# Joint last column tiles of two projections, rows reloaded into places that come free, and other places for the sample steps, in a one-core decoder layer on Trainium2

## The chip, the cores and the metric

The kernel runs on one core of one Trainium2 chip. The metric is the device time of one execution in microseconds (us). Execution is launched once; everything below happens inside it.

A core has TensorE (PE in the profile, its weight loads PEld), VectorE (DVE), ScalarE (ACT), GpSimd (POOL) and SyncE (SP). Each engine runs its own program in order; they meet through semaphores, with `wait_ge` on one side and `then_inc` on the other. DMA transfers are issued from an engine's queue and signal a semaphore when they land.

## The reference, cut to what matters

All data is float32. There are 1024 prompt rows and 8 sample rows, together R = 1032 rows of D = 2048 columns.

```python
h = rms_norm(x, g_mix);  z = h @ w_in
oa = three dilated windows of 16 heads, mixed by their softmax denominators
ob = sliding window of 128 keys, 16 query / 4 kv heads, sink logits
y = concat(oa * silu(ga), ob * silu(gb))                   # 2048 columns
h = x + y @ w_out
gate = sigmoid(rms_norm(h, g_ple) @ w_pg)
out = rms_norm(h + (p @ w_ple) * gate, g_final)            # p has 256 columns
# the 8 sample rows attend to caches: cache_a (2048 positions), cache_b (128 positions)
```

w_in has 6656 columns, that is NZ = 52 tiles of 128; `ORDER` lists them in the order in which they are computed.

## The kernel before, in words

**Products.** Each product of float32 matrices is made of three products of rounded parts: an activation tile is split into a high part (`act_hi`, rounded) and a low part (`act_lo`, the rest), and so is each weight. `three()` (line 809) issues for one k (one of KT = 16 row blocks of the weights) the products hi*hi, lo*hi and hi*lo of 344 rows into a PSUM bank. The 1032 rows are three stretches of 344 (t = 0, 1, 2), so a column tile is 3 x 16 x 3 = 144 products. A pair (tile, t) is a unit. The step of one k of one unit is a position: position 16u + k.

**Weights.** SP loads a group of four k of a tile (256 KB) into one of two raw places (`weights(g)`, line 261); GpSimd rounds it and subtracts (lines 575 and 577) into one of five places of a ring (`WRING`). It waits for the place to be used up. There are 208 groups for w_in and 64 for w_out. The gate's weights w_pg and w_ple have places of their own (`u_even`, `u_odd`, line 229), are loaded a whole tile at a time (`load_u`, line 519) and are split by VectorE (`split_u`, line 1381).

**First projection** (line 818). Units run one after the other through PSUM banks 0 and 1. ScalarE copies a unit out (line 948) or, for the 16 gating tiles from unit GATE0 = 108 on, takes its silu (line 955); VectorE multiplies that by the attention output (line 1311) and SP stores the product to DRAM (`yt_scratch`, line 457).

**Work beside it.** The attention of the prompt, the sample rows' attention A (`sa`, eight sequences) and B (`sb`) run between the products of the first projection. The table in `events()` (line 68) says at which position each step stands. Every engine walks the same list in order of position (`ALONG`): TensorE executes a step's matmuls when it reaches the position, SP issues that step's loads, VectorE and ScalarE do their parts. So a step's wait on TensorE holds up all later products, and a step's wait on SP holds up all later loads. For each sequence b of sample attention A the steps stand at 1448 + 96b plus an offset: key and value loads (`sa_load`, line 386), VectorE's scores (`sk`, line 1225), TensorE's steps 1 to 5 (`sa_step`, line 723). For attention B the rows are turned at 2226, TensorE turns each sequence's scores at 2250 + 14b as VectorE delivers them (line 779), and the steps 1 to 4 stand at 2370, 2400, 2420 and 2440. The projection ends at position 2496.

**Second projection** (line 840). When the last unit's y is stored, SP loads all 16 row blocks of y back into four places (`y_in`, line 502), ScalarE rounds each (line 1062), VectorE subtracts (line 1364), and TensorE computes tile 0 with k outermost, behind them. Tiles 1 to 15 then run unit by unit. Every unit ends with three small matmuls that add the residual x (`residual`, line 833). ScalarE copies h out and stores it (line 1071); VectorE adds up the squares of h over the 16 tiles in `acc` (lines 1369 and 1371).

**Gate stage.** After the last tile: TensorE sums `acc` over the partitions with a matrix of ones (line 870), VectorE adds eps (1376), ScalarE takes the root (1077), VectorE inverts (1379). Meanwhile SP loads h back (line 528), ScalarE scales and rounds (1081), VectorE subtracts (1390), and in between TensorE turns the nine row tiles of p (line 877). Then each of 16 column tiles has three units of 48 + 6 products (gate, then embedding, lines 886 to 888) and a turn of the previous unit's result (line 898); VectorE and ScalarE form h + ple * gate, and GpSimd issues the stores to `y_scratch` (lines 584 and 585).

**Last stage.** SP loads nine row tiles of y (line 552) into three places; ScalarE squares, VectorE scales into one of two places `f_out`, GpSimd issues the store of the output (line 589). ScalarE's next square but one into the same place waits for that store.

## Time and profile before

| | us |
|---|---|
| median of 3 runs | 2685.92 (2680.72 to 2686.15) |
| the profiled execution's own time | 2688.74 |
| its span, first to last instruction | 2686.9 |
| PE busy | 2468.8 (92%) |
| DVE, ACT, POOL busy | 861.3, 610.3, 621.5 |
| mean granted TensorE clock | 0.958 |

The span is that of the profiled execution. Products overlap in the pipeline, so the duration shown for one is longer than the distance from one start to the next; the distance is what counts. The stretches of the span are: up to 66 us the input norm and turn; 66 to 1727.6 the first projection; 1727.6 to 1767.6 the first tile of the second; to 2138.8 its other tiles; to 2190.6 the way into the gate stage and its first unit; to 2604.9 the gate stage; then the last stage.

### The profile page before, as it was taken

To read this page: it belongs to the slowest core of one execution; us is meant where nothing else is said; L and a number is where in the kernel's file an instruction comes from. 1 tells how busy PE (TensorE), PEld (TensorE's weight loads), DVE (VectorE), ACT (ScalarE), POOL (GpSimd) and SP (SyncE) were. 2 spreads that over 40 slices of the span, in tenths; PEclk is the share of its full clock that TensorE was granted. 3 is DMA by queue.
4 is the path that set the end of the run, shared out by engine and by line. 5 is a ranking of instruction groups with operands and counts; after the bars stand their busy time and mean duration, and the time that the engine had idled before them with its cause. 6 is when DMAs were issued, how large, how long until landed. Compare 5 with 4: busy or idle time off the path is not lost.

```text
span 2686.9 us, 40432 instructions
## 1 busy us (share of the span) xinstructions
PE 2468.8 (92%) x16617; PEld 2298.9 (86%) x16617; DVE 861.3 (32%) x2136; ACT 610.3 (23%) x1458; POOL 621.5 (23%) x653
## 2 busy tenths in 40 slices
PE   4999999999999999999899887899999969999970
PEld 3998888888888898888788887799999859999970
DVE  7022332332332304445544223231101163323224
ACT  5022222222222213335454000120000131101013
POOL 2222222222222232222111321234333201111110
PEclk7999999999999999999999998899999979999995
DMA  4132222232322234434443442443323253232326
GB/s 170 57 117 93 87 91 91 91 97 85 96 90 83 70 99 133 136 112 131 143 121 116 130 142 76 135 145 95 89 75 90 78 184 96 73 96 74 94 70 235
DMA packets 301962, 287.95 MB, mean 107 GB/s; under 512 B 20865, under 2 KB 267449, under 8 KB 298425
## 3 DMA queue, kind: packets, MB, share of 16 engines
q1 hardware_dynamic: 278898, 241.11, 29.8%
q10 hardware_dynamic: 17856, 27.34, 3.0%
q0 software_dynamic: 5024, 16.92, 1.7%
q8 instruction: 132, 2.16, 0.3%
q14 instruction: 52, 0.43, 0.1%
HBM read 215.48 MB, written 69.81 MB: 106 GB/s over the span
## 4 chain that ended last, share of the span: by engine, by line
PE 83%; DVE 7%; DMA 6%; ACT 2%; issue 1%; POOL 1%; SPq 1%; POOLq 0%; DVEq 0%; ACTq 0%
PE psum L813 18%; PE psum L815 17%; PE psum L814 17%; PE psum L886 5%; PE psum L888 5%; PE psum L887 5%; PE psum L618 3%; PE psum L634 3%; PE psum L646 3%; DMA s_ring<-in_cache_a_v 1%; PE psum L837 1%; DMA out<-f_out 1%; PE psum L674 1%; DMA s_ring<-in_cache_a_k 1%; PE psum L689 1%
## 5 line engine op out<-in xcount | busy, mean ns | idle before, releaser
L813 PE MATMUL psum<-act_hi,w_hi 128*128 128x344 f32 x3264 | 1078.9, 331 | 14.1 <-DVE act_lo L1364 13.1
L815 PE MATMUL psum<-act_hi,w_lo 128*128 128x344 f32 x3264 | 1051.9, 322 | 0.0
L814 PE MATMUL psum<-act_lo,w_hi 128*128 128x344 f32 x3264 | 1051.5, 322 | 0.0
L813 PEld LDWEIGHTS psum<-act_hi,w_hi 128*128 128x128 f32 x3264 | 623.6, 191 | 25.7 <-issue 20.1
L814 PEld LDWEIGHTS psum<-act_lo,w_hi 128*128 128x128 f32 x3264 | 622.7, 191 | 0.0
L815 PEld LDWEIGHTS psum<-act_hi,w_lo 128*128 128x128 f32 x3264 | 622.1, 191 | 0.0
L575 POOL CAST w_hi<-w_raw 128x512 fp32r<-128x512 f32 x272 | 182.4, 671 | 1547.9 <-PE psum L815 1406.6
L577 POOL TENSOR_TENSOR w_lo<-w_raw,w_hi 128x512 fp32r<-128x512 f32 x272 | 366.5, 1348 | 21.8
L1162 DVE COPY prob_t<-psum 128x512 f32<-128x512 f32 (+2 forms) x96 | 53.5, 558 | 470.0 <-PE psum L646 470.0
L584 POOL DMA_DIRECT2D y_scratch<-y_nat x48 | 36.7, 764 | 425.1 <-ACT y_nat L1092 415.5
L886 PE MATMUL psum<-act_hi,u_even 128*128 128x344 f32 x384 | 125.5, 327 | 9.4 <-DVE u_even L1387 8.3
L970 ACT ACTIVATE prob<-prob,mx 128x256 f32<-128x256 f32 (+7 forms) x128 | 98.4, 770 | 145.8 <-DVE mx L1190 145.8
L1184 DVE CUSTOM_DVE_ANT_0 prob<-psum,bias 128x512 f32<-128x512 f32 (+2 forms) x192 | 98.7, 552 | 94.9 <-PE psum L618 94.9
L964 ACT ACTIVATE prob_t<-psum 128x512 f32<-128x512 f32 (+2 forms) x96 | 47.2, 492 | 353.6 <-PE psum L646 353.6
L1369 DVE TENSOR_TENSOR sq<-h_row 128x1032 f32<-128x1032 f32 x16 | 21.3, 1332 | 326.9 <-ACT h_row L1071 326.9
L886 PE MATMUL psum<-act_hi,u_odd 128*128 128x344 f32 x384 | 124.6, 325 | 0.0
L888 PE MATMUL psum<-act_hi,u_even 128*128 128x344 f32 x384 | 123.1, 321 | 0.0
L887 PE MATMUL psum<-act_lo,u_even 128*128 128x344 f32 x384 | 123.0, 320 | 0.0
L888 PE MATMUL psum<-act_hi,u_odd 128*128 128x344 f32 x384 | 122.5, 319 | 0.0
L887 PE MATMUL psum<-act_lo,u_odd 128*128 128x344 f32 x384 | 122.5, 319 | 0.0
L1095 ACT ACTIVATE t_gate<-t_gate 128x344 f32<-128x344 f32 x48 | 23.6, 492 | 374.0 <-DVE t_gate L1407 374.0
L1407 DVE TENSOR_TENSOR t_gate<-psum,acc 128x344 f32<-128x344 f32 x48 | 24.8, 517 | 252.4 <-PE psum L888 252.4
(198 smaller groups left out, 2742.1 us busy)
## 6 DMA issues: line engine op xcount, KB each, us to landing
w_raw<-in_w_in SPq DMA_DIRECT2D x208, 256.0 KB, 3.0
w_raw<-in_w_out SPq DMA_DIRECT2D x64, 256.0 KB, 2.8
u_raw<-in_w_pg SPq DMA_DIRECT2D x16, 1024.0 KB, 6.3
z_scratch<-stage ACTq DMA_DIRECT2D x72, 172.0 KB, 1.8
h_scratch<-h_row ACTq DMA_DIRECT2D x16, 516.0 KB, 3.3
h_stage<-h_scratch SPq DMA_DIRECT2D x16, 516.0 KB, 4.7
h_in<-h_scratch SPq DMA_DIRECT2D x48, 172.0 KB, 2.6
x_in<-in_x_prompt SPq DMA_DIRECT2D x8, 1024.0 KB, 5.1
```

The lines of the kernel that those rows point to most:

```text
L575: pool.tensor_copy(w_hi[:, slot], w_raw[:, g % 2]).then_inc(sem("w_rounded"), 1)
L577: pool.tensor_tensor(w_lo[:, slot], w_raw[:, g % 2], w_hi[:, slot].bitcast(F32), ALU.subtract).then_inc(sem("w_split"), 1)
L618: pe.matmul(psum[:, 2 + h, 0:nk], zq[half, b * BLK:(b + 1) * BLK], zk[half, n_ % 2, k0:k0 + nk], start=True, stop=True).then_inc(sem("a_sc ...
L634: mm = pe.matmul(psum[HD * h:HD * h + HD, 6, (b % 4) * P:(b % 4 + 1) * P], v_nat[:, k0 // P + x, HD * h:HD * h + HD], prob_t[:, h, x * P:( ...
L813: pe.matmul(psum[:, bank, 0:T3], w_hi[:, slot, x, :], act_hi[:, k, rows], start=(k == 0), stop=False, skip_group_check=True)
L814: pe.matmul(psum[:, bank, 0:T3], w_hi[:, slot, x, :], act_lo[:, k, rows], start=False, stop=False, skip_group_check=True)
L815: return pe.matmul(psum[:, bank, 0:T3], w_lo[:, slot, x, :], act_hi[:, k, rows], start=False, stop=stop, skip_group_check=True)
L886: pe.matmul(psum[:, bank, 0:T3], hi_w[:, first + k, :], hi_a[:, k, rows], start=(k == 0), stop=False, skip_group_check=True)
L887: pe.matmul(psum[:, bank, 0:T3], hi_w[:, first + k, :], lo_a[:, k, rows], start=False, stop=False, skip_group_check=True)
L888: mm = pe.matmul(psum[:, bank, 0:T3], lo_w[:, first + k, :], hi_a[:, k, rows], start=False, stop=(k == tiles - 1), skip_group_check=True)
L970: act.activation(pr, pr, ACT.Exp, bias=mx[:, b % 4, 4 + h:5 + h], accum_out=mx[:, b % 4, 6 + h:7 + h]).then_inc(sem("a_exped"), 1)
L1184: dve.tensor_tensor_reduce(prob_of(n, b)[:, h, k0:k0 + nk], psum[:, 2 + h, 0:nk], bias[:, h, u0:u0 + nk], SCALE, -3e38, ALU.add, ALU.max, ...
```

## The change

**Joint tiles.** The last two tiles of the first projection, and the last two of the second, are computed with k outermost: for each k both tiles, all three stretches, in six PSUM banks. When both have used a k of the old activations, a semaphore (`x_used`, `yk_used`) says so, and ScalarE and VectorE write the reloaded rows of the next stage into that place of `act_hi` and `act_lo`. So 14 of the 16 blocks of y are reloaded while the pair of the first projection runs, and 14 of h while that of the second runs; the last two come from PSUM and from `h_row` directly, not through DRAM. `y_in` and `h_stage` have three places instead of four.

**Sample steps.** The pair needs banks 0 to 5, so the sample attention has to be over at position 2400 (`sb_done`). Steps of A stand at 1448 + 88b with other offsets; B's begin at 2160; TensorE turns all eight sequences' scores together at step 1 (position 2330), with one wait. Steps 2 to 4 stand at 2350, 2366 and 2382.

**Weights.** All weights, w_pg and w_ple too, go through GpSimd's ring of five as one list of groups (`GROUPS`, `USES`); a tile of the gate stage has four groups of four k and one of two. VectorE's split is gone.

**Gate stage.** Tile 0 is computed with k outermost in banks 4 to 6. The sums over the partitions come within it (after k = 11 and k = 14). The turns of p are put behind tiles 1 to 9 of the second projection. Turned results go to banks 3 and 7.

**Queues.** The stores of `y_scratch` and of the output are issued by ScalarE instead of GpSimd. The load of `g_ple` (4-byte elements) moves from before the gate stage to the kernel's beginning, ahead of `g_mix`.

```diff
@@ events
-    for b in range(NB):
-        first = 1448 + 96 * b
-        for i, at in enumerate((0, 1, 14, 18, 30, 76)):
+        first = 1448 + 88 * b
+        for i, at in enumerate((0, 1, 16, 22, 34, 72)):
             put(first + at, "sa_load", b, i)
-        for t, at in enumerate((8, 13, 24)):
+        for t, at in enumerate((8, 13, 26)):
             put(first + at, "sk", b, t)
-        for step, at in ((1, 34), (2, 54), (3, 72), (4, 84), (5, 94)):
+        for step, at in ((1, 42), (2, 58), (3, 70), (4, 83), (5, 87)):
             put(first + at, "sa", b, step)
-    put(2226, "sb_rows")
-    put(2240, "sb", 0)
-        put(2250 + 14 * b, "sb_seq", b)
-    put(2370, "sb", 1)  # 2400, 2420, 2440: 2, 3, 4
+    put(2160, "sb_rows")
+    put(2174, "sb", 0)
+        put(2184 + 14 * b, "sb_seq", b)
+    put(2330, "sb", 1)  # 2350, 2366, 2382: 2, 3, 4
@@ TensorE
+            pe.wait_ge(sem("bank_free"), ZPAIR)
+            pe.wait_ge(sem("sb_done"), 1)
+            for k in range(KT):
+                for i in range(2):
+                    group_wait("in", NZ - 2 + i, k)
+                    for t in range(3):
+                        mm = three(3 * i + t, "in", NZ - 2 + i, k, t, k == KT - 1)
...
+                    if k < KT - 1 and i == 1:
+                        mm.then_inc(sem("x_used"), 1)
...
+                if k == 11:
+                    pe.wait_ge(sem("h_summed"), 3 * KT)
+                    mean_square(0)
+                    mean_square(1)
+                elif k == 14:
+                    pe.wait_ge(sem("h_eps"), 1)
+                    mean_square(2)
@@ ScalarE
+            for k in range(HPAIR):
+                act.wait_ge(sem(f"y_loaded{k % 3}"), 16 * (k // 3 + 1))
+                act.wait_ge(sem("x_used"), k + 1)
+                act.activation(act_hi[:, k, 0:S], y_in[:, k % 3, :], ACT.Copy).then_inc(sem("y_hi"), 1)
+            act.wait_ge(sem("y_split"), HPAIR)
+            for j in range(2):
+                act.wait_ge(sem("produced"), ZPAIR + 3 * j + 3)
+                act.activation(gs[:, HPAIR + j, :], psum[:, 3 * j + 2, S - 2 * T3:T3], ACT.Silu).then_inc(sem("gs_gated"), 1)
...
+                act.wait_ge(sem("f_scaled"), i + 1)
+                act.dma_start(yp[r0:r0 + n, :] if i < 8 else ys, f_out[0:n, i % 2, :]).then_inc(sem(f"out_stored{i % 2}"), 16)
@@ GpSimd
-            for g in range(WG * NT):
+            for g, (what, i, k, n) in enumerate(GROUPS):
...
-                pool.dma_start(y_dram[q0:q0 + 256, n * P:(n + 1) * P].rearrange("(c p) n -> p c n", p=P), y_nat[:, u % 2, 0:2, :]).then_inc(sem(f"y_stored{u % 2}"), 16)
```

## Rows read from the trace of the kernel before

**Rows 1.** Stretch, length; busy PE, PEld, DVE, ACT, POOL; clock, DMA share, GB/s.

```profile
1050.00:1556.00 506.00, 477.42 (x3302) 420.63 (x3301) 221.03 (x759) 196.99 (x523) 115.11 (x120) 0.97 0.43 126
1556.00:1705.00 149.00, 123.32 (x759) 118.77 (x758) 44.17 (x81) 11.88 (x25) 35.81 (x38) 0.91 0.35 108
1727.60:1767.60 40.00, 26.86 (x145) 25.32 (x145) 25.24 (x22) 17.48 (x18) 8.20 (x7) 0.83 0.82 264
2138.80:2190.60 51.80, 19.84 (x79) 14.40 (x80) 36.76 (x35) 25.38 (x31) 0.00 (x0) 0.60 0.79 246
2190.60:2604.90 414.30, 414.30 (x2679) 413.47 (x2679) 133.63 (x171) 42.56 (x137) 68.04 (x90) 1.00 0.28 80
2604.90:2686.90 82.00, 0.91 (x7) 0.39 (x5) 30.16 (x57) 22.92 (x35) 8.61 (x15) 0.52 0.62 226
```

**Rows 2.** TensorE's waits: line, releaser, us in total, times, longest.

```profile
PE psum L779 <- DVE bsc L1334: 19.5, 6, 7.1
PE psum L719 <- DMA s_ring<-in_cache_a_v: 14.6, 8, 3.7
PE psum L727 <- DVE s_sc L1239: 10.3, 5, 3.2
PE psum L785 <- DVE bprob L1303: 6.2, 1, 6.2
```

**Rows 3.** Timeline of TensorE, products after a wait: start, duration.

```profile
1577.10 0.49 PE L814 MATMUL psum<-act_lo,w_hi 128*128 128x344 f32 x1
1577.39 0.49 PE L815 MATMUL psum<-act_hi,w_lo 128*128 128x344 f32 x1
...
1680.56 0.32 PE L814 MATMUL psum<-act_lo,w_hi 128*128 128x344 f32 x1
1680.71 0.32 PE L815 MATMUL psum<-act_hi,w_lo 128*128 128x344 f32 x1
```

**Rows 4.** Chain of waits: a value load of sample attention A.

```profile
1410.83 3.88 DMA s_ring<-in_cache_a_v
```

**Rows 5.** Groups of instructions: count, busy, mean ns, idle before.

```profile
L577 POOL TENSOR_TENSOR w_lo<-w_raw,w_hi 128x512 fp32r<-128x512 f32 x272 | 366.5, 1348 | 21.8
L575 POOL CAST w_hi<-w_raw 128x512 fp32r<-128x512 f32 x272 | 182.4, 671 | 1547.9 <-PE psum L815 1406.6 <-DMA w_raw<-in_w_in 113.2 <-DMA w_raw<-in_w_out 27.4
L1379 DVE RECIPROCAL acc<-acc 128x344 f32<-128x344 f32 x3 | 6.6, 2262 | 0.0
L877 PE MATMUL psum<-ident,y_nat 128*128 128x128 f32 (+1 forms) x18 | 5.8, 423 | 19.4 <-DMA y_nat<-in_p_prompt 12.6 <-DVE pt_lo L1394 5.6 <-DMA y_nat<-in_p_sample 1.2
L870 PE MATMUL psum<-acc,ones 128*128 128x344 f32 x6 | 3.8, 808 | 3.2 <-DVE acc L1371 3.2
L1360 DVE CAST act_hi<-ystmp 128x128 fp32r<-128x128 f32 x1 | 1.2, 1243 | 0.0
```

**Rows 6.** Timeline: first and last reloaded block of y.

```profile
1736.86 2.17 ACT L1062 ACTIVATE act_hi<-y_in 128x1024 fp32r<-128x1024 f32 x2 [8.64 <-DMA y_in<-yt_scratch]
...
1764.83 1.23 DVE L1364 TENSOR_TENSOR act_lo<-y_in,act_hi 128x1024 fp32r<-128x1024 f32 x1 [1.10 <-ACT act_hi L1062]
```

**Rows 7.** Last stage, chain of waits: start, duration, what.

```profile
2620.31 2.00 ACT f_out L1105 x2
...
2636.92 2.01 ACT f_out L1105 x2
...
2642.86 8.86 DMA out<-f_out
2651.80 2.01 ACT f_out L1105 x2
...
2673.76 2.36 DVE f_out L1422
```

**Rows 8.** The same view as rows 1, within the last stage.

```profile
2632.00:2637.00 5.00, 0.00 (x0) 0.00 (x0) 0.00 (x0) 0.08 (x1) 0.00 (x0) 0.50 0.99 411
```

**Rows 9.** The load of `g_ple`: issue to landing.

```profile
DMA to landing us min/median/max: 3.0/3.0/3.0
```

More of the change, by code:

```diff
@@ L65, with weight_groups, group_uses @@
 WRING = 5
+ZPAIR = 3 * (NZ - 2)
+HPAIR = KT - 2
+def weight_groups():
+    parts = range(0, KT, WG)
+    out = [("in", i, k, WG) for i in range(NZ - 2) for k in parts] + [("in", NZ - 2 + i, k, WG) for k in parts for i in range(2)]
+    out += [("out", i, k, WG) for i in range(HPAIR) for k in parts] + [("out", HPAIR + i, k, WG) for k in parts for i in range(2)]
+    for n in range(KT):
+        out += [("gate", n, k, WG) for k in parts] + [("ple", n, 0, 2)]
+    return out
+GROUPS = weight_groups()
+GROUP = {(what, i, k): g for g, (what, i, k, _) in enumerate(GROUPS)}
+def group_uses():
+    out, count = [], 0
+    for what, i, k, n in GROUPS:
+        if what == "in" and k + n == KT:
+            out.append(("produced", 3 * i + 3))
+        elif what == "in" and i == NZ - 1:
+            out.append(("x_used", k + n))
+        elif what == "out" and i == KT - 1:
+            out.append(("yk_used", k + n))
+        elif what == "ple":
+            out.append(("u_produced", 3 * i + 3))
+        else:
+            count += 1
+            out.append(("w_used", count))
+    return out
+USES = group_uses()
 def events():
@@ new lines, in _ @@
+            load_x_cols(0)
+            weights(first + 13)
+            weights(first + 14)
+            first = GROUP["out", 0, 0]
+            for i in range(HPAIR):
+                load_x_cols(i + 1)
+                if i < len(ROW_TILES):
+                    r0, n = ROW_TILES[i]
+                    if i == 0:
+                        sp.wait_ge(sem("y_split"), HPAIR + 6)
+                    if i >= 2:
+                        sp.wait_ge(sem("p_turned"), i - 1)
+                    sp.dma_start(p_nat[0:n, i % 2, :], p_p[r0:r0 + n, :] if i < 8 else p_s).then_inc(sem(f"p_loaded{i % 2}"), 16)
+                for part in range(WG):
+                    weights(first + WG * i + part + 7)
@@ new lines, in _ @@
+            load_x_cols(KT - 1)
+            first = GROUP["out", HPAIR, 0]
+            for k in range(HPAIR):
+                if k >= 3:
+                    sp.wait_ge(sem("h_split"), k - 2)
+                sp.wait_ge(sem(f"h_stored{k % 2}"), 16 * (k // 2 + 1))
+                sp.dma_start(h_stage[:, k % 3, :], h_dram[k]).then_inc(sem(f"h_loaded{k % 3}"), 16)
+                if k % WG == 1 and k > WG:
+                    weights(first + 2 * (k // WG) + 5)
+                    weights(first + 2 * (k // WG) + 6)
@@ new lines, in _ @@
+            pe.wait_ge(sem("h_bank_free"), 3 * HPAIR)
+            for k in range(KT):
+                for i in range(2):
+                    group_wait("out", HPAIR + i, k)
+                    for t in range(3):
+                        mm = three(h_banks[i][t], "out", HPAIR + i, k, t, False)
+                    if i == 1:
+                        mm.then_inc(sem("yk_used"), 1)
+                    elif k % WG == WG - 1:
+                        mm.then_inc(sem("w_used"), 1)
+            residual(HPAIR)
@@ new lines, in _, with mean_square, embedding @@
+            residual(HPAIR + 1)
+            turn_bank = (3, 7)
+            def mean_square(t):
+                pe.matmul(psum[:, turn_bank[t % 2], 0:T3], ones[:], acc[:, T3 * t:T3 * (t + 1)], start=True, stop=True).then_inc(sem("h_meaned"), 1)
+            def embedding(n, t):
+                for k in range(2):
+                    if t == 0:
+                        group_wait("ple", n, k)
+                    mm = three(t, "ple", n, k, t, k == 1, pt_hi, pt_lo)
+                mm.then_inc(sem("u_produced"), 1)
@@ L911, in _ @@
-                    mm.then_inc(sem("u_produced"), 1)
-                    if u >= 1:
+                    pe.wait_ge(sem("p_read"), u - 2)
+                    for k in range(KT):
+                        if t == 0:
+                            group_wait("gate", n, k)
+                        mm = three(4 + t, "gate", n, k, t, k == KT - 1)
+                        if t == 2 and k % WG == WG - 1:
+                            mm.then_inc(sem("w_used"), 1)
+                    embedding(n, t)
+                    if u == 3:
+                        y_turn(0)
+                        y_turn(1)
+                    elif u == 4:
+                        y_turn(2)
+                        y_turn(3)
+                    else:
```

444 lines of the change are left out of this document (226 added, 218 removed).

## The prediction

> **What bounds the kernel now.** I read the busy time by stretch first [rows 1]. In the gate stage (2190.6 to 2604.9) TensorE is busy all of the time at a granted clock of 1.00: nothing but fewer products would shorten it. It loses time in five places: sample attention A beside the first projection (1050 to 1556, 477.4 busy of 506), sample attention B (1556 to 1705, 123.3 of 149), the first tile of the second projection (26.9 of 40), the way into the gate stage (19.8 of 51.8), and the last stage (82 us, nearly without it). Second view, TensorE's waits [rows 2]: line 779 waits 19.5 us in six times for VectorE's scores, line 719 14.6 in eight for value loads, line 727 10.3 in five, line 785 6.2 once. Third, what comes after a wait [rows 3]: behind the 7.1 us wait of line 779 products start 0.29 us apart; later, 0.157 apart (1680.56 to 1680.71; mean of 9068 such distances). The granted clock in these stretches falls below 1.00 [rows 1], so this is the 1.2 GHz level against 2.4. A slow product costs 0.13 us. I counted the distances of 0.27 to 0.31: 74 in stretch A (9.5 us), 65 in stretch B (8.4 us; first and last in [rows 3]).
>
> **The change, part by part.**
>
> *Steps of B: gain 33.* Before, TensorE waits for each of eight scores, 14 positions apart (14 x 3 x 0.157 = 6.6 us), while VectorE is held by loads that SP issues in order behind its stores. Now it waits once, at 2330, 156 positions (73.6 us) after the first q rows are asked for; before, the whole series of eight took about 70 us, TensorE's own waits included. So the 19.5 go. Step 2 follows step 1 by 20 positions plus eight turns, 10.6 us; softmax and its exponentials need about 11 (before they needed the same, but began 6 us late, behind the silu of the unit at 2400). Of 6.2 remains about 0.6. With 8.4 us of slow products: 34.1 lost before, 1 after. Bounds 20 to 34: if the series is late as before, the 14 us of lines 779 and 785 that its last third causes stay.
>
> *Steps of A: gain 30.* Line 727 (VectorE's third score) got 10 positions behind the score's own place, now 16; with the attention steps between, a position takes about 0.69 us there, so 4 us more against waits of at most 3.2: gone. Line 719 waits for the third value load. It stood at +76, always the place of a weight load, whose wait for GpSimd (0.67 + 1.35 us, [rows 5]) held SP; the step came 8 positions later (5.5 us), against 2.0 + 0.5 + 3.9 [rows 4] = 6.4. Now it is 11 positions (7.6 us), and with 88 instead of 96 positions per sequence only two of eight still fall on a weight load's place: 3 us remain of 14.6. With the slow products, 14.6 + 10.3 + 9.5 = 34.4 lost, 4 after. Bounds 0 to 34: steps 4 and 5 are now 4 positions apart, and a late VectorE would show at once; the loads of one sequence are nearer to the next's.
>
> *First projection into second: gain 13.* The stretch takes 40.0 us and does 144 products, 22.6 us: 17.4 lost. After: TensorE waits at the pair's beginning for both banks, one silu: 1.0. The pair lasts 288 x 0.157 = 45.3 us. SP must first issue six loads of the attention output and then the first y: landed about 10 us after the last unit. Blocks then followed at 1.8 us each with four places (1736.86 to 1764.83 for sixteen, [rows 6]); with three places I take 2.3: one load of about 4 us, ScalarE 1.1, VectorE 1.2, issues, over three. Fourteen are done at 10 + 2.4 + 13 x 2.3 = 42, before the pair's end at 46.3. At the end the sample columns are still serial: silu, product, cast 1.24 [rows 5], rest: 3.0 us, of which 0.9 is covered by the two stretches that need them not. So 1.0 + 2.1 + 1.0 for slow products = 4.1 lost; gain 13.3. Bounds 3 to 16; at 2.65 us a block the cover ends, at 3.3 it costs 9 us.
>
> *Second projection into gate: gain 31.* Of 51.8 us, unit 0 (54 x 0.157 = 8.5) is work: 43.3 lost. After: h is reloaded beneath the second pair (45.3 us for fourteen blocks, as above, and SP comes to it 3 us in). TensorE keeps the three sums with ones (3.8 at the low clock in [rows 5], 1.9 at full) and the turns of p (5.8 at the low clock, about 3.3). The last sum comes after k = 14 of tile 0, 23.1 us in; then eps 0.5, three reciprocals on VectorE of 2.26 [rows 5], then gate product, sigmoid, product: the bank is read at 32.2, while TensorE has tile 0 and its embeddings done at 27.4. A new wait of 4.9 us, and 2.0 of slow products behind it (as after waits of 4 us). The squares of the last two tiles are summed by about 10 us, before k = 11 at 17. With 0.3 for a bank: 12.4 lost, gain 30.9. Bounds 20 to 35.
>
> *Weights of the gate through GpSimd: 0.* A group takes 2.0 us, 4.5 groups a tile: 9 of 26.4 us. The ring of five is exactly one tile. The first place comes free at k = 3 of the third unit, 12 k x 0.47 + embedding 0.9 + a turn 0.3 = 6.9 us before it is needed, filled in 2.0. Later groups have more. Cover gone only if a split takes over 6.9.
> The Trainium skill speaks against this move: "SBUF — State Buffer", "SBUF: two separate sides", calls the port pair of VectorE and GpSimd an exclusive lock, where the loser waits for the whole instruction. VectorE's instructions in that loop are 0.5 us long, so by rule a group gains 1 us at most, well within 6.9.
>
> *Queues, last stage: gain 6.* ScalarE issues the store, so it can't square ahead: square to store takes 2636.92 to 2642.86, 5.9 us, plus the issue 0.4: 6.35 per tile, if the store lands within 6.7. Before, two tiles took 14.9 (2636.92 to 2651.80), because a store took about 9 [rows 7]: four transfers of 1 MB were in flight together. Staggered, two are: 2 MB at the 411 GB/s that the DMA engines move when busy all the time [rows 8], 5.1 us, plus 1.6 of latency (estimate). From the first square 2620.3 to the last full tile's scaling 2673.8 are 53.5; after 1.3 + 7 x 6.35 + 3.5 = 49.3. Plus 1 at the start (stores issued sooner) and 0.8 at the end. Bounds -3 to 9.
>
> *g_ple at the beginning: loss 1.* It landed in 3.0 us alone [rows 9]; now it stands ahead of the first x and costs an issue and a share of it. Bounds 0 to 3. VectorE's squares in stretches of 344, turned results in other banks, more ones of residual at a tile's end: nothing, since VectorE works 34% of the gate stage.
>
> Sum: 33 + 30 + 13.3 + 30.9 + 6 - 1 = 112. From the profiled execution's own 2688.7: 2576.5. That execution is 2.8 above the median; I predict 2576.
>
> **The rivals.**
> 1. *The sample steps of A wait as before.* For: closer steps, one SP in order; nothing in the trace shows them so dense. Against: each slack above grew. Then 30 come back: 2606.
> 2. *The reloads don't fit beneath the pairs*, at 3.3 us a block with three places, in competition with weights: 1736.9 to 1764.8 had a DMA share of 0.82 [rows 1] with other loads absent. Price 9 each: 2594. Against: the pair gives 2.65 a block, four places needed 1.8.
> 3. *The last stage gets slower.* If a store keeps its 8.9 us [rows 7], squares follow by (5.9 + 8.9)/2 = 7.4 us, but in strict turn: 1.3 + 7 x 7.4 + 3.5 = 56.6, so 3 lost instead of 4 gained: 2583. The Trainium skill has that rule: "DMA: Bandwidth & Descriptors", "Issuing engines are not separate DMA queues", says that all queues run on the same 16 DMA engines, so that another issuing engine saves hardly more than issue time.
> 4. *Slower than before: GpSimd's ring starves the gate stage.* The place is the first products of each of 15 tiles, which wait for a group that is freed 6.9 us ahead. Price 15 x (s - 6.9) for a split time s including load and SP's queue, where SP waits for `h_added` between weights. To eat 112 us it takes s = 14.4, against 2.0 + a load of 3. For: everything of the loads now stands in one order. Against: DMA share is 0.28 there, and raw places are filled ahead.
> 5. *The copy beneath the pair isn't what ends the stretch* (the change does not do what it says): the semaphores free a k only when both tiles used it; if ScalarE were behind for other reasons, both transitions would stay: -44 of gain, 2620.
>
> **How the numbers follow.** Forecast 0.62, rivals 1 0.14, 2 0.09, 3 0.08, 4 0.03, 5 0.04. The likeliest one's own range is 2560 to 2592 (the bounds of the terms, not all on one side). To leave out no more than 2 in 10, rivals 1 to 3 are taken in: 2556 to 2608. A change of under 0.2% (5 us) can't be told from none. Faster by more than that: all cases but 4 and a small rest, 0.96; within 0.01; slower 0.03.
>
> **What would show it.** TensorE's waits: no more than 1 us for the scores of B, under 4 us for value loads, the third score's wait gone; a new wait of about 5 us at the first product of gate unit 3, for VectorE; about 2 us at the first products of the second projection for VectorE's sample columns. Granted clock 1.00 between 1556 and the end of the second projection but for one spell. ScalarE's copies of y end before the first pair's last product. Squares in the last stage 6.3 apart. It would be wrong if waits for `w_split` show up in the gate stage, if y is copied after the pair, or if stretch A keeps its 10 us for line 727.

## The result and the profile after

| | before | after |
|---|---|---|
| median | 2683.32 us (2679.86 to 2686.15, 4 runs) | 2593.79 us (2590.08 to 2596.2, 4 runs) |
| span of the profiled execution | 2686.9 | 2591.1 |
| mean granted TensorE clock | 0.958 | 0.974 |

The ratio is 0.9666, 95% interval [0.9647, 0.9685]: 89.5 us less at the medians, 95.8 between the two profiled spans, since the profiled execution of the kernel before (2688.74) was 5.4 us above its median. Forecast: 2576 in a range of 2556 to 2608.

First view, the windows of the changed kernel: sample attention A, sample attention B with the joint pair behind it, the second projection's first tile, the gate stage from the last small product of the second projection on, and the last stage from the last product of the gate stage on. Columns as in [rows 1]. Against the fourth line here stand two lines there, 51.8 + 414.3 = 466.1 us, since the gate's first tile is now one piece.

```profile
1040.00:1516.00 476.00, 457.86 (x3230) 400.96 (x3229) 224.56 (x780) 201.33 (x536) 110.36 (x112) 0.98 0.44 131
1516.00:1684.50 168.50, 164.55 (x1070) 160.93 (x1069) 71.56 (x97) 26.86 (x43) 56.00 (x54) 0.99 0.52 165
1684.50:1710.60 26.10, 23.24 (x138) 23.27 (x139) 8.73 (x17) 3.96 (x10) 8.18 (x9) 0.93 0.26 76
2084.20:2515.40 431.20, 426.67 (x2737) 425.10 (x2737) 93.73 (x159) 49.32 (x145) 131.80 (x150) 0.99 0.28 81
2515.40:2591.10 75.70, 0.94 (x7) 0.42 (x5) 30.34 (x57) 23.14 (x35) 0.00 (x0) 0.53 0.67 244
```

Stretch A still loses 18 of 476 us, stretch B 4 of 168.5. The first tile takes 26.1 us where it took 40.0, the gate stage 431.2 where it took 466.1, and it starts without a gap; the last stage takes 75.7 instead of 82.0.

Second view, TensorE's waits in the changed kernel (line, releaser; us, times, longest), against [rows 2], with the lines that matter here.

```profile
PE psum L716 <- DVE mx L1339: 10.1, 4, 3.9
PE psum L855 <- DVE t_y L1544: 4.5, 1, 4.5
PE psum L761 <- DMA s_ring<-in_cache_a_v: 3.9, 2, 3.6
PE psum L855 <- DVE act_lo L1489: 2.9, 1, 2.9
PE psum L744 <- DVE prob_b L1327: 2.5, 1, 2.5
PE psum L855 <- POOL w_lo L631: 2.4, 1, 2.4
...
PE psum L827 <- DVE bprob L1423: 0.9, 1, 0.9
...
PE psum L769 <- DVE s_sc L1359: 0.6, 1, 0.6
```

The 19.5 us for B's scores are gone, the value loads fell from 14.6 to 3.9, the third score's wait from 10.3 to 0.6 (line 769), the one wait of 6.2 in attention B to 0.9 (line 827, forecast 0.6). Forecast as new were 4.9 (now 4.5, `t_y`) and 2.1 (2.9, `act_lo` line 1489). Not forecast: 12.6 us at lines 716 and 744, the products and turns of *prompt* attention B, and 2.4 at a weight group. The kernel before lost little at the same products:

```profile
PE psum L674 <- DVE mx L1219: 2.6, 3, 1.8
```

Third view, TensorE in order of time behind the 4.5 us wait: products 0.29 us apart, then 0.16, as in [rows 3]. Such slow products stand in the trace behind several waits, so a wait costs more than itself.

```profile
2115.90 0.66 PE L855 MATMUL psum<-act_hi,w_hi 128*128 128x344 f32 x1 [4.53 <-DVE t_y L1544]
...
2120.65 0.49 PE L856 MATMUL psum<-act_lo,w_hi 128*128 128x344 f32 x1
2120.94 0.45 PE L857 MATMUL psum<-act_hi,w_lo 128*128 128x344 f32 x1
...
2121.39 0.32 PE L856 MATMUL psum<-act_lo,w_hi 128*128 128x344 f32 x1
2121.55 0.32 PE L857 MATMUL psum<-act_hi,w_lo 128*128 128x344 f32 x1
```

### The profile page after: what moved, and what is told of

Same layout as the page of the kernel before. It is cut to its first block, busy times and chain, and to the rows that moved or that the text cites. A ratio compares the mean times of both kernels' runs of the same rounds, so it can differ in the third digit from the quotient of the medians.

```text
span 2591.1 us, 40760 instructions
## 1 busy us (share of the span) xinstructions
PE 2445.8 (94%) x16617; PEld 2284.7 (88%) x16617; DVE 816.9 (32%) x2172; ACT 611.4 (24%) x1462; POOL 676.7 (26%) x708
## 4 chain that ended last, share of the span: by engine, by line
PE 87%; DVE 6%; DMA 4%; ACT 2%; issue 1%; SPq 1%; POOL 0%; ACTq 0%; DVEq 0%; POOLq 0%
PE psum L855 24%; PE psum L857 23%; PE psum L856 23%; PE psum L660 3%; PE psum L676 3%; PE psum L688 3%; PE psum L716 1%; PE psum L900 1%; DMA s_ring<-in_cache_a_k 1%; PE psum L731 1%; PE psum L744 1%; DMA out<-f_out 1%; DVE x_n L1259 1%; DVE act_lo L1251 1%; DVE s_prod L1352 1%
## 5 line engine op out<-in xcount | busy, mean ns | idle before, releaser
L855 PE MATMUL psum<-act_hi,w_hi 128*128 128x344 f32 x4032 | 1319.1, 327 | 11.9 <-DVE t_y L1544 4.5
L857 PE MATMUL psum<-act_hi,w_lo 128*128 128x344 f32 x4032 | 1292.2, 320 | 0.0
L856 PE MATMUL psum<-act_lo,w_hi 128*128 128x344 f32 x4032 | 1291.6, 320 | 0.0
L855 PEld LDWEIGHTS psum<-act_hi,w_hi 128*128 128x128 f32 x4032 | 763.0, 189 | 22.0 <-issue 10.9
L856 PEld LDWEIGHTS psum<-act_lo,w_hi 128*128 128x128 f32 x4032 | 762.4, 189 | 0.2
L857 PEld LDWEIGHTS psum<-act_hi,w_lo 128*128 128x128 f32 x4032 | 762.0, 189 | 0.0
L629 POOL CAST w_hi<-w_raw 128x512 fp32r<-128x512 f32 (+1 forms) x352 | 224.6, 638 | 1789.4 <-PE psum L857 1625.4
L631 POOL TENSOR_TENSOR w_lo<-w_raw,w_hi 128x512 fp32r<-128x512 f32 (+1 forms) x352 | 456.7, 1297 | 28.2
L660 PE MATMUL psum<-zk,zq 64*128 64x512 f32 (+3 forms) x384 | 88.0, 535 | 0.0
L676 PE MATMUL psum<-prob_t,v_nat 128*64 128x128 f32 x1152 | 84.1, 281 | 0.0
```

The costliest lines, as they stand in the source:

```text
L629: pool.tensor_copy(w_hi[:, slot, 0:n], w_raw[:, g % 2, 0:n]).then_inc(sem("w_rounded"), 1)
L631: pool.tensor_tensor(w_lo[:, slot, 0:n], w_raw[:, g % 2, 0:n], w_hi[:, slot, 0:n].bitcast(F32), ALU.subtract).then_inc(sem("w_split"), 1)
L660: pe.matmul(psum[:, 2 + h, 0:nk], zq[half, b * BLK:(b + 1) * BLK], zk[half, n_ % 2, k0:k0 + nk], start=True, stop=True).then_inc(sem("a_sc ...
L676: mm = pe.matmul(psum[HD * h:HD * h + HD, 6, (b % 4) * P:(b % 4 + 1) * P], v_nat[:, k0 // P + x, HD * h:HD * h + HD], prob_t[:, h, x * P:( ...
L855: pe.matmul(psum[:, bank, 0:T3], w_hi[:, slot, x, :], hi_a[:, k, rows], start=(k == 0), stop=False, skip_group_check=True)
L856: pe.matmul(psum[:, bank, 0:T3], w_hi[:, slot, x, :], lo_a[:, k, rows], start=False, stop=False, skip_group_check=True)
```

## What the first forecast missed, seen in the trace

Line 716 waits for a score bank that line 1339 on VectorE empties. VectorE came to that late because it had stood, in order, in front of a score of sample attention A, whose keys had not landed. VectorE's wait for keys between 1000 and 1520 us, and its timeline ahead of TensorE's wait of 3.36 us at 1348.18. After its 4.29 us in front of the score it had the scores of that sequence, a gating product and two smaller steps to do before it came to the bank:

```profile
DVE s_prod L1352 <- DMA s_ring<-in_cache_a_k: 37.2, 8, 8.0
```

```profile
1338.03 0.69 DVE L1352 TENSOR_TENSOR s_prod<-s_ring,s_q 128x512 f32<-128x512 f32 x1 [4.29 <-DMA s_ring<-in_cache_a_k]
...
1344.74 1.43 DVE L1431 TENSOR_TENSOR stage<-stage,o_in 128x344 f32<-128x344 f32 x1
...
1347.61 0.42 DVE L1339 CUSTOM_DVE_ANT_0 prob_b<-psum,bias_b 128x256 f32<-128x256 f32 x1
```

```profile
1348.18 0.74 PE L716 MATMUL psum<-zkb,zq 64*128 64x128 f32 x4 [3.36 <-DVE mx L1339]
```

The kernel before waited for keys at the same score (its line 1232) for only 6.1 us in 5 times:

```profile
its engine sat idle before it (us, times) until:
  DMA s_ring<-in_cache_a_k: 6.1, 5
```

In both kernels the first score stands 8 positions (5.5 us) behind its load in the table. What differs is when SyncE comes to it. SyncE (SPq: the engine issues) and VectorE at the second sequence, in the changed kernel:

```profile
1059.90 9.09 SPq L306 DMA_DIRECT2D w_raw<-in_w_in  x4
...
1076.79 0.69 DVE L1352 TENSOR_TENSOR s_prod<-s_ring,s_q 128x512 f32<-128x512 f32 x1 [7.97 <-DMA s_ring<-in_cache_a_k]
```

The chain of waits of the same stretch goes from GpSimd's split of a weight group over SyncE's weight load, q rows and keys to VectorE, and from there to TensorE's wait of 2.46 us at 1081.78:

```profile
1067.31 1.29 POOL w_lo L631
1068.62 0.37 SPq L306
1069.09 0.60 SPq L434
1069.74 6.96 DMA s_ring<-in_cache_a_k
...
1081.29 0.33 DVE prob_b L1339
...
1081.78 0.95 PE psum L716 x3
```

And the second sequence in the kernel before:

```profile
1060.88 5.98 SPq L266 DMA_DIRECT2D w_raw<-in_w_in  x3
1066.96 0.96 SPq L393 DMA_DIRECT2D s_q<-q_scratch  x1
1067.97 0.91 SPq L403 DMA_DIRECT2D s_ring<-in_cache_a_k  x2
...
1075.94 0.69 DVE L1232 TENSOR_TENSOR s_prod<-s_ring,s_q 128x512 f32<-128x512 f32 x1 [0.64 <-DMA s_ring<-in_cache_a_k]
```

The flight is alike, 7.05 and 7.97 us from issue to use. But VectorE was ready 7.3 us after the issue before (1075.30), and 0.9 us ahead of it after (1068.82). With 88 positions the second sequence begins at 1536, which is also the place of a tile's fourth weight load; that load waits for GpSimd's split of its raw place, and the q rows and keys stand behind it. With 96, twice a tile's 48, every sequence begins at the same place of a tile (8), away from weight loads. Of the four first-score waits over 1 us after (7.97, 4.36, 4.29, 7.61) three belong to the sequences 1, 2 and 7, which begin at a weight load's position (1536, 1624, 2064). At the fourth (4.29) SyncE came to the keys at 1332.32, behind its store of a unit's y at 1330.96.

## Experiments

Differences of two kernels are between medians; a ratio to before has an interval of 0.0013 to 0.002 to each side, so a difference between two kernels is known to 5 to 7 us.

**1. Only the new places of sample attention A** (`b_a_places`, the kernel before with one edit):

```diff
-        first = 1448 + 96 * b
-        for i, at in enumerate((0, 1, 14, 18, 30, 76)):
+        first = 1448 + 88 * b
+        for i, at in enumerate((0, 1, 16, 22, 34, 72)):
...
-        for t, at in enumerate((8, 13, 24)):
+        for t, at in enumerate((8, 13, 26)):
...
-        for step, at in ((1, 34), (2, 54), (3, 72), (4, 84), (5, 94)):
+        for step, at in ((1, 42), (2, 58), (3, 70), (4, 83), (5, 87)):
```

> The kernel before with only the new places of sample attention A (88 instead of 96 positions a sequence and the new offsets). Theory: the gain of stretch A in the changed kernel (28.6 us of waits and 9.5 of slow products before, 18.3 and 4.3 after: 15.6) comes from these places alone, so about 15 us faster than before (2668), with the waits for VectorE's third score gone, value waits under 5 us, and new waits at the score products of prompt attention B (about 10 us). Rival 1: the places bring all of the 30 us I had forecast and the changed kernel loses half of it to something else it changed (2653). Rival 2: the places bring nothing and the gain came from elsewhere (2683).

Measured: 2680.57 us (2671.74 to 2683.39, 11 runs), ratio 0.9988 [0.9979, 0.9997]: 2 us, nearest to rival 2. I had expected 2668. Its trace shows why: the waits for values fell, and one at the score products took their place (14.1 us, against 2.6 before).

```profile
PE psum L674 <- DVE mx L1219: 14.1, 6, 4.5
...
PE psum L719 <- DMA s_ring<-in_cache_a_v: 4.1, 3, 3.6
```

**2. The new places of A and B, one turn of B's scores** (`b_ab_places`, the same and:)

```diff
-        put(2250 + 14 * b, "sb_seq", b)
+        put(2184 + 14 * b, "sb_seq", b)
...
+                    pe.wait_ge(sem("sb_scored"), NB)
+                    for b in range(NB):
+                        mm = pe.transpose(psum[0:HEADS, 2 + b // 4, P * (b % 4):P * (b % 4 + 1)], bsc[:, b, :], ident[:])
+                    mm.then_inc(sem("sb_rowed"), 1)
```

> The kernel before with the new places of both sample attentions and with one turn of B's eight scores behind one wait, no joint tiles. Theory: the two gains add and need no joint tiles: 15.6 for A and 29.3 for B, 45 us faster than before (2638); TensorE's waits for B's scores under 2 us. Rival: B's gain hangs on the shorter projection behind it (weights for fewer single tiles, SP's queue), then B gives less than 20 here (2650 or more).

Measured: 2652.17 us (2641.49 to 2656.14, 5 runs), ratio 0.9878 [0.986, 0.9897]: 30.7 us, so 28 for B and 2 for A. That is the time of the rival (2650 or more), but not for its reason: B gave what was expected of it and A did not. At the median the sample steps gave half of the 63 us of the forecast; the runs lie 15 us apart. Its trace (2645.28 us) has 39.2 us of VectorE waiting for keys and 12.9 at line 674.

**3. The scores of A six positions later** (`a_scores_later`, the changed kernel with):

```diff
-        for i, at in enumerate((0, 1, 16, 22, 34, 72)):
+        for i, at in enumerate((0, 1, 18, 24, 36, 72)):
...
-        for t, at in enumerate((8, 13, 26)):
+        for t, at in enumerate((14, 20, 30)):
```

> The changed kernel with VectorE's scores of sample attention A at +14, +20, +30 instead of +8, +13, +26 and the loads behind them at +18, +24, +36. Theory: VectorE, in order, stands in front of these scores for the key loads (36.5 us in 7 waits) and so frees prompt attention B's score banks late; TensorE loses 12.6 us at these products and turns and 4.3 behind them at the slow clock. With 6 positions more (4.1 us) most key waits are under 4 us and TensorE's waits at the score products fall from 10.1 to under 3: 8 to 13 us faster than the changed kernel (about 2583). Rival 1: the loads are simply too dense for the queue, the waits move to step 1 (line 769) or the value products (line 761): no change, 2590 to 2598. Rival 2: VectorE's own backlog holds the banks, not the loads: the waits of line 716 stay at 7 or more while the key waits fall.

Measured: 2574.56 us (2572.57 to 2576.63, 4 runs), ratio to before 0.9595 [0.9582, 0.9608], 19 to 21 us faster than the changed kernel (2593.79; 2595.36 when it ran again in experiment 6). Both rivals fall: line 716 dropped from 10.1 to 1.7, and little took its place (the value loads rose from 3.9 to 5.0). The size was more than I expected. Between ScalarE's copies of units 90 and 149 TensorE's idle time fell from 21.8 to 11.5 us, and its slow products from 45 to 8 (4.8 us); that is 15 of the 18 us gained between these two events. The other 3 were not taken apart.

```profile
PE psum L716 <- DVE mx L1339: 1.7, 2, 1.1
```

```profile
DVE s_prod L1352 <- DMA s_ring<-in_cache_a_k: 18.5, 7, 5.9
```

**4. The loads sooner instead** (`a_keys_sooner`, the changed kernel with the scores left where they are):

```diff
-        for i, at in enumerate((0, 1, 16, 22, 34, 72)):
+        for i, at in enumerate((-5, -4, 16, 22, 34, 72)):
```

> The changed kernel with the q rows and the first two key loads of each sequence of A asked for five positions sooner (-5 and -4 instead of 0 and 1), the scores left at +8, +13, +26. Theory: what counts is the distance from the load to the score, not where the score stands beside TensorE's steps; in the trace of the changed kernel SyncE came to these loads 0.9 us after VectorE stood ready, held by a weight load at the same position. Five positions are 3.4 us: VectorE's waits for keys fall from 37 us to about 20 and line 716 from 10 to under 4, 12 us faster than the changed kernel (2582); the third key load, unmoved, keeps its waits (12 us in three). Rival: the place of the scores was what mattered (they stood right in front of the bias steps), then the gain is under 4 us; or SyncE, which now waits for the sequence before to give up its value places, holds weight loads behind it, and it is slower.

Measured: 2578.41 us (2573.44 to 2581.53, 5 runs), 0.9607 [0.9587, 0.9627]: 15 to 17 us faster. VectorE's waits for keys fell to 11.5, of which 10.2 are the third block's, unmoved:

```profile
PE psum L716 <- DVE mx L1339: 4.3, 2, 3.9
```

So it is the distance from load to score that counts, from whichever side it is made. Beside experiment 3 the trace has a second wait for a weight group (4.7 us in 2); that SyncE's earlier waits bring it is not shown.

**5. Later scores without joint tiles** (`b_ab_later`: experiment 2 with the diff of 3).

> The kernel before with the new places of both sample attentions and the scores of A at +14, +20, +30. Theory: what the joint tiles do has no part in the missed gain, so the later scores bring their 19 us here as well: 2633, and the sample steps then give 50 of the 63 us of my forecast. Rival: without the joint tiles something else holds A (the sample steps alone gave only 31 us at the median, 12 less than in the profiled run): under 10 us, 2643 or more.

Measured: 2625.54 us (2622.35 to 2627.88, 5 runs), ratio 0.9783 [0.9769, 0.9797]: 26.6 us less than experiment 2. Its wait at line 674 is 2.8 us in 3, against 12.9 in experiment 2. The sample steps then give 57 of the 63 us forecast. How the time runs along the projection is seen in the start of ScalarE's copy of a unit, in us after that of unit 0:

| unit | before | exp. 1 | exp. 2 | after | exp. 3 | exp. 5 |
|---|---|---|---|---|---|---|
| 90 | 934.2 | 934.2 | 934.3 | 934.3 | 934.2 | 934.3 |
| 108 | 1137.1 | 1140.3 | 1140.6 | 1138.2 | 1131.6 | 1132.0 |
| 120 | 1284.5 | 1292.5 | 1291.1 | 1288.9 | 1274.9 | 1275.9 |
| 132 | 1422.7 | 1422.4 | 1421.2 | 1416.7 | 1399.4 | 1400.5 |
| 149 | 1594.1 | 1583.0 | 1564.4 | 1559.6 | 1541.3 | 1541.8 |

Up to unit 120 the kernels with the new places and the early scores are 4 to 8 us behind the one before, and those with the later scores 9 to 10 ahead. Not all of the first figure is loss: at 88 positions a sequence more of A's steps lie ahead of unit 120. TensorE's idle time and slow products from unit 90 to 120 are 18.6 us before, 20.8, 20.4 and 19.2 in experiments 1 and 2 and the changed kernel, 7.5 and 9.2 in experiments 3 and 5. So with the early scores the new places gained nothing there.

The joint tiles and the rest of the change were worth 58 us with the early scores (experiment 2 to the changed kernel) and 51 with the later ones (experiment 5 to 3); the forecast has 49 for them. The 7 us between are hardly more than such a difference is known to, and no run explains them.

**6. The changed kernel again** (`after_again`), beside the two that follow.

> The changed kernel itself, on the chip of the three that follow. All theories: 2588 to 2597, since its four runs lay between 2590.1 and 2596.2.

Measured: 2595.36 us (2588.75 to 2598.53, 5 runs).

**7. The covers** (`a_covers`, the changed kernel with two orders changed on TensorE):

```diff
-                if k == 11:
+                if k == 7:
...
-                elif k == 14:
+                elif k == 9:
@@ out tile 0
+                steps = [(k, t) for k in range(KT) for t in range(3)]
+                if i == 0:
+                    steps = [(k, t) for k in range(WG) for t in range(2)] + [(k, 2) for k in range(WG)] + steps[3 * WG:]
```

> The changed kernel with two orders of TensorE changed: the sums over the partitions after k = 7 and k = 9 of the gate's first tile instead of k = 11 and 14, and in the first tile of the second projection the third stretch of the first four k behind the two others. Theory: VectorE's three reciprocals (6.6 us) end 5.7 us sooner, so the wait of 4.5 before gate unit 3 and the 2.2 of slow products behind it go; the 2.9 for the sample columns is covered by 16 more products (2.5 us), of it and its 1.55 of slow products about 0.5 remains. Together 10 us faster (2584): about 6.5 and 4. Rival 1: the sums come too early, VectorE has not added the squares of the last tile after k = 7 (its last square ended 8 us into the tile, k = 7 ends 12 in): a new wait of 2 to 5 us there. Rival 2: the wait of unit 3 moves to unit 4 or 5, since VectorE then has three units to catch up on: gain under 3.

Measured: 2585.63 us (2582.62 to 2589.37, 4 runs), 0.9637 [0.9624, 0.965]: 8 to 10 us faster; the spans are 10.3 apart. Between 1680 and 2130 us TensorE has one wait left, 0.5 us for ScalarE, where the changed kernel had 2.9 and 4.5 for VectorE.

**8. Two places for the reloads** (`a_two_places`, the changed kernel; for `h_stage` alike):

```diff
-                if k >= 3:
-                    sp.wait_ge(sem("y_split"), k - 2)
-                sp.dma_start(y_in[:, k % 3, :], yt_dram[k]).then_inc(sem(f"y_loaded{k % 3}"), 16)
+                if k >= 2:
+                    sp.wait_ge(sem("y_split"), k - 1)
+                sp.dma_start(y_in[:, k % 2, :], yt_dram[k]).then_inc(sem(f"y_loaded{k % 2}"), 16)
```

> The changed kernel with two places for the reloaded rows of y and of h instead of three. Theory: in the changed kernel fourteen blocks of y came 2.37 us apart with three places and were ready 2.5 us before the pair's end, so the cover is nearly used up. With two, a block takes half of a load (5.2), both casts (1.1 + 1.2) and the issue: 3.6 us; the last is ready about 14 us after the pair's end, ScalarE's silus of banks 0 to 5 come behind it, and TensorE waits at the third stretch of tile 0 for bank 0: 12 to 16 us at the first transition and about 8 at the second, together 20 to 24 us slower (2614). Rival: the DMA engines set the 2.37 us, not the places; then two places do as well and it costs under 3 us (2595).

Measured: 2607.64 us (2601.65 to 2609.36, 4 runs), 0.972 [0.9705, 0.9735]: 12 us slower than the changed kernel beside it, where I had expected 20 to 24. First and last cast of y with three places (the changed kernel), then with two:

```profile
1650.11 1.06 ACT L1153 ACTIVATE act_hi<-y_in 128x1024 fp32r<-128x1024 f32 x1 [12.17 <-DMA y_in<-yt_scratch]
...
1680.96 1.06 ACT L1153 ACTIVATE act_hi<-y_in 128x1024 fp32r<-128x1024 f32 x1 [1.37 <-DMA y_in<-yt_scratch]
```

```profile
1652.69 1.07 ACT L1153 ACTIVATE act_hi<-y_in 128x1024 fp32r<-128x1024 f32 x1 [12.18 <-DMA y_in<-yt_scratch]
...
1693.78 1.06 ACT L1153 ACTIVATE act_hi<-y_in 128x1024 fp32r<-128x1024 f32 x1 [2.21 <-DMA y_in<-yt_scratch]
```

```profile
PE psum L855 <- DVE act_lo L1489: 12.6, 1, 12.6
```

Over thirteen distances that is 2.37 us a block against 3.16. The first transition costs what I expected (12.6), the second nothing: its last h blocks came at 2096.22, after the pair's last products, but behind them the gate's first tile needs one k each 1.4 us, and the bank was free in time. So the places set the pace, as forecast, and I counted the cover of the second transition too low.

**9. Output stores issued by GpSimd again** (`a_pool_out`, the changed kernel):

```diff
@@ ScalarE
-                act.wait_ge(sem("f_scaled"), i + 1)
-                act.dma_start(yp[r0:r0 + n, :] if i < 8 else ys, f_out[0:n, i % 2, :]).then_inc(sem(f"out_stored{i % 2}"), 16)
@@ GpSimd
+            for i, (r0, n) in enumerate(ROW_TILES):
+                pool.wait_ge(sem("f_scaled"), i + 1)
+                pool.dma_start(yp[r0:r0 + n, :] if i < 8 else ys, f_out[0:n, i % 2, :]).then_inc(sem(f"out_stored{i % 2}"), 16)
```

> The changed kernel with the nine stores of the output issued by GpSimd again, as before. Theory: ScalarE can then square ahead, two tiles' loads and stores are in flight together, and the last stage takes 79 us as before instead of 72.9: 5 to 6 us slower than the changed kernel (2598). Rival: the 6.3 us came from the order around it (the y stores, the load of g_final), not from who issues the output; then 0 (2593).

Measured: 2594.97 us (2592.64 to 2599.99, 4 runs), 0.968 [0.9665, 0.9694]: no difference that these runs can tell (0.4 less, known to about 6). The traces can: the squares of tiles 2 and 4, first with GpSimd, then of the changed kernel.

```profile
2543.34 1.91 ACT L1227 ACTIVATE f_out<-f_in 128x2048 f32<-128x2048 f32 x1 [9.46 <-DMA out<-f_out]
...
2559.04 1.91 ACT L1227 ACTIVATE f_out<-f_in 128x2048 f32<-128x2048 f32 x1 [9.21 <-DMA out<-f_out]
```

```profile
2543.51 1.91 ACT L1223 ACTIVATE f_out<-f_in 128x2048 f32<-128x2048 f32 x1 [4.90 <-DMA out<-f_out]
...
2557.02 1.91 ACT L1223 ACTIVATE f_out<-f_in 128x2048 f32<-128x2048 f32 x1 [4.92 <-DMA out<-f_out]
```

Two tiles take 15.7 us against 13.5, and from the first square to the end of the span it is 66.8 (2526.84 to 2593.6) against 62.1 (2528.97 to 2591.1): 4.6 of the 6.3 us gained in the last stage go with who issues. All traces agree: from the first square to the end it is 62.0 to 62.9 us in the nine kernels in which ScalarE issues these stores, and 66.6 to 67.7 in the five in which GpSimd does. Executions of one kernel lie 6 to 10 us apart, which is why the medians don't show it.

**10. The parts together** (`a_best`: experiments 3 and 7, and SyncE asks for B's q rows one sequence later):

```diff
-                elif e[0] == "sb_seq" and e[1] + 2 < NB:
-                    b = e[1] + 2
+                elif e[0] == "sb_seq" and 1 <= e[1] and e[1] + 1 < NB:
+                    b = e[1] + 1
```

> The changed kernel with the later scores, the two covers, and the q rows of sample attention B asked for one sequence later by SyncE, so that it does not stand in front of weight loads for VectorE's scores. Theory: the parts lie in different stretches and add: 19 for the scores, 8 for the covers, 2 to 4 for the wait of 2.4 us for weights at the head of a tile beside B and the slow products behind it: 2563. Rival: with VectorE and TensorE closer together after the first part, the others' waits were partly the same time (each hidden wait gives the clock and DMA less slack): 2570 or more.

Measured: 2562.47 us (2561.44 to 2566.59, 4 runs), 0.9559 [0.9546, 0.9572]. That is 31 to 33 under the changed kernel, where the parts alone gave 19 to 21 and 8 to 10: they add. But the wait for weights stayed: 2.83 us. The timeline of all engines shows the chain: SyncE asks for q rows; VectorE waits 6.72 for them and only then multiplies the unit's y (at 1521.07); SyncE's store of it waits, the weight load stands behind that store, and GpSimd waits 7.83 for the weights.

```profile
1511.94 0.83 SPq L517 DMA_DIRECT2D q_ring<-q_scratch  x2
...
1515.83 3.95 DVE L1403 TENSOR_TENSOR bprod<-kb,q_ring 128x256 f32<-128x256 f32 x4 [6.72 <-DMA q_ring<-q_scratch]
...
1521.61 0.32 SPq L498 DMA_DIRECT2D yt_scratch<-stage  x1
...
1522.45 0.46 SPq L306 DMA_DIRECT2D w_raw<-in_w_in  x1
...
1527.00 0.61 POOL L629 CAST w_hi<-w_raw 128x512 fp32r<-128x512 f32 x1 [7.83 <-DMA w_raw<-in_w_in]
```

**11. B's series later, A's third value load sooner** (`a_best2`, experiment 10 with):

```diff
-        put(2184 + 14 * b, "sb_seq", b)
+        put(2198 + 14 * b, "sb_seq", b)
...
-        for i, at in enumerate((0, 1, 18, 24, 36, 72)):
+        for i, at in enumerate((0, 1, 18, 24, 36, 70)):
...
-        for step, at in ((1, 42), (2, 58), (3, 70), (4, 83), (5, 87)):
+        for step, at in ((1, 42), (2, 58), (3, 68), (4, 84), (5, 88)):
```

> The best so far with two more changes of places: sample attention B's series of scores begins at 2198 instead of 2184 (VectorE then does not stand in front of q rows that SyncE asked for just before, with the gating product and SyncE's store and weight loads behind it), and in A the third value load goes to +70 behind step 3 at +68, with step 4 at +84 and step 5 at +88. Theory: the wait for a weight group beside B (2.8 and 1.2 of slow products) goes, and of 5.7 for value loads (and 0.9 of slow products) 2 remain: 2555. Rival: the weight group is late for another reason than VectorE's hold, its wait stays, and the values are late because the queue is full, not because they are asked for late: 2562.

Measured: 2553.68 us (2553.0 to 2555.8, 4 runs), 0.9515 [0.9502, 0.9529]: the fastest, 129 us under before and about 40 under the changed kernel. The waits for weights and values are both gone from its list, whose largest entry behind the input norm is 2.0 us in 3 at line 716. The two edits were not run apart.

**12. The scores four positions later still** (`a_best3`, experiment 11 with 22, 28, 38 for the loads, 18, 24, 34 for the scores, step 1 at 43):

> The same with the scores of A later still, +18, +24, +34 (loads +22, +28, +38, step 1 at +43). Theory, taken on: each position between a key load and its score takes VectorE's waits down until they are zero; 18.5 us of them were left at +14, TensorE lost only 2.7 to them, so 1 to 2 us faster than the kernel beside it (2554). Rival: the slack in front of step 1 (9 positions instead of 12) is used up and its wait (line 769) grows: 3 to 8 us slower (2560).

Measured: 2558.65 us (2558.46 to 2559.48, 4 runs), 0.9533 [0.952, 0.9546]: 5 us slower, in runs beside those of experiment 11 that do not overlap with them. The rival was right. VectorE waits no more for keys, and TensorE waits for VectorE's third score again, as in the kernel before: step 1 now stands 9 positions behind it, where the changed kernel has 16 and experiment 11 has 12:

```profile
PE psum L769 <- DVE s_sc L1362: 5.2, 3, 2.9
```

## Why the prediction was right, and where it was not

| term of the sum | forecast | traces before and after |
|---|---|---|
| steps of B | 33 | 28.7 |
| steps of A | 30 | 15.6 |
| first projection into second | 13.3 | 13.9 |
| second projection, behind its first tile, into gate stage | 30.9 | 32.5 |
| last stage | 6 | 6.3 |
| `g_ple` at the beginning | -1 | -1.3 |

The terms of A and B are waits and slow products of TensorE in their stretches (A: 28.6 + 9.5 before, 18.1 + 4.4 after; B: 34.1 and 5.4); the others are distances between the same events (last product of the first projection, first small product of line 837 or 900, last product of the gate stage). The sum of the right column is 95.7, and the spans differ by 95.8. At the medians it is 89.5, and there experiment 1 gives 2 us and not 15.6 for the places of A: part of the right column is the slower execution that was profiled before.

*The number.* 2593.79 lies in the stated range, but 1.8 us above the 2560 to 2592 of the likeliest case alone; rivals 1 to 3 had widened it. The transitions and the last stage came within 2 us of their terms; the sample steps fell 18.7 us short of theirs, and the time is 17.8 above the forecast. So the other terms were right, and the error of A was caught by the width of the range. The last step has a small slip: 2688.7 less 112.2 is the time of the profiled execution, and its 2.8 us above the median were not taken off.

*Steps of A: the step that failed.* The term of 30 took it that nothing but TensorE's own waits on A's steps holds the stretch. I weighed the slack of TensorE's steps (lines 719 and 727) and found each grown; that was right, both waits fell as said. I did not weigh the slack of VectorE's own step, the score 8 positions behind its load, (I had asked which *value* loads fall on a weight load's place, two of eight, and not which key loads do), nor what is queued behind it on VectorE: the bias step of prompt attention B, for which TensorE waits. My text named the danger ("the loads of one sequence are nearer to the next's") and gave it a bound, not a place. Experiment 3 shows the cause, since six more positions between load and score return 19 to 21 us; 4 makes the distance from the other side; 5 shows that it needs no joint tiles; 12 shows that the scores can't go much later, because step 1 then waits for them. That a weight load's place is what made SyncE late is read from the chain of waits and from the positions; no run moved that alone.

*Steps of B.* Right but for 4.3 us: the wait of 2.4 for weights with 1.4 of slow products, which is gone in experiment 11, and small ones. I had treated one wait on TensorE as the end of the matter and not followed SyncE, which waits for VectorE there.

*The transitions.* The pace of y was 2.37 us a block (forecast 2.3). VectorE's last subtraction ended at 1683.29, 1.2 us before the pair's end at 1684.5 (forecast 4). Rival 2 did not come true, but experiment 8 shows how near it is: one place fewer costs 12. *Gate.* The wait before unit 3 was 4.5 (forecast 4.9); experiment 7 shows that it hangs on when the sums start. The clock was to be at its full level from 1556 us on but for one spell; there were two of 11 slow products each, behind the wait for weights (1544.0) and behind the sample columns (1687.36).

*Weights through GpSimd.* Nothing, as forecast: between 2084.2 and 2515.4 us TensorE waits for no weight group, with GpSimd busy for 131.8 of 431.2 us. Rival 4 is out. (VectorE's share of the gate stage before, given as 34%, is 133.6 of 414.3 us in [rows 1], 32%.)

*Last stage.* The 6 us came, and 4.6 of them with the queue (experiment 9). A tile took 6.8 us (2528.97 to 2576.53 for seven) and not 6.35, since the squares stand 7.3 and 6.1 apart in turn: every second one waits 4.9 for a store. The forecast let a store take 6.7, of which 1.6 was a latency that no row gives; the first one here was issued at 2535.75, and the square that waits for it starts at 2543.51, 7.8 later. The Trainium skill, "DMA: Bandwidth & Descriptors", "Issuing engines are not separate DMA queues", says that another issuing engine saves only its issue time. The traces here show more than that: with these stores on ScalarE the last stage is 4 to 5 us shorter (experiment 9). My reading is that the transfers don't run elsewhere, but that a store issued by ScalarE keeps ScalarE from squaring ahead, so fewer transfers are in flight together: the squares stand 7.3 and 6.1 us apart instead of in pairs, and a store lands in 6.2 us at the median instead of the 9.1 of experiment 9. No run held ScalarE back and left the stores with GpSimd.

*Rivals.* Of rival 1 (all of A stays, 0.14) half happened by the traces and nearly all by experiment 1, by another wait than those I had named. Rival 3 (the last stage slower, 0.08) and 5 (the transitions stay, 0.04) did not come.

## What to carry to other kernels

When steps on several engines are placed by hand, check the slack of each engine's own waits, not only those of the engine that is the bound: an engine with 32% busy time can still hold it by standing in order in front of a load. Both sides of a distance cost something: here the score 8 positions behind its load cost about 20 us against 14, and at 18, with too little room in front of the next step, 5 us. So measure two or three values. And a new cover (a reload beneath other work) is worth a run with one place less, which tells how much is left of it.

## What was not expected of the hardware

Requests closer together did not make a load slower. Where VectorE stood waiting for the first keys of a sequence, they took 5.7 to 7.5 us from issue to use with 88 positions a sequence and 6.7 to 8.9 with 96. Not every wait of TensorE was followed by slow products: behind 2.46 us at line 716 (1081.78) eleven products were slow, behind 2.51 at line 744 (1470.77) none; behind waits under 1.4 us, from unit 90 on, none were in these two traces.
